# Splitting the mid-kernel loads of a gather-bound layer into transfers of 120 and 8 partitions

## What is computed

```python
h = rmsnorm(x, norm1_g) * (1 + sc1) + sh1
z = h @ w_in                                   # token mixer: SSM and short convolution
x = x + g1 * (mix(z) @ w_out)
h = rmsnorm(x, norm2_g) * (1 + sc2) + sh2
# PEER, per block of 128 tokens: 8 heads, 16 experts of 16384 for each head and token
q = h @ w_query                                # 256 columns for each head
idx, gate = product_key_top_k(q, sub_keys)
hid = einsum("thkd,td->thk", expert_u[idx], h)
act = gelu(hid) * gate
x = x + g2 * einsum("thk,thkd->td", act, expert_v[idx])
y = rmsnorm(x, final_norm_g)
```

## Time and profile before

| | us |
|---|---|
| three runs | 1945.32, 1943.67, 1938.72 |
| median | 1943.67 |
| profiled execution | 1940.8 |
| its span, first to last instruction | 1939.0 |

### The profile page before, as it was taken

One profiled execution on the slowest core, in us unless ns is written; L12 is line 12 of the kernel. 1 busy time (PEld: TensorE's weight loads), 2 busy tenths in 40 slices (PEclk: granted clock), 3 DMA queues, 4 the chain that ended last, 5 costly groups with the idle time before them and its releaser, 6 DMA issues.

```text
span 1939.0 us, 22593 instructions
## 1 busy us (share of the span) xinstructions
PE 1193.7 (62%) x7716; PEld 472.6 (24%) x7716; DVE 1417.4 (73%) x3894; ACT 373.2 (19%) x845; POOL 721.3 (37%) x666
## 2 busy tenths in 40 slices
PE   6999898999767777774643434454444454444434
PEld 3569544444323322220210000111000010110001
DVE  8978567777766776669777777777777778877775
ACT  5242441221122121111210011121111021111010
POOL 0000133333433343435444444444444444444441
PEclk9999999999878777775655555575555565555555
DMA  8555799999999999999999999999999999999994
GB/s 348 182 198 210 274 392 404 371 385 415 403 417 393 403 411 417 409 404 398 421 421 423 421 421 421 421 420 420 423 418 413 421 412 401 420 419 415 413 416 192
DMA packets 126243, 745.91 MB, mean 385 GB/s; under 512 B 12128, under 2 KB 34912, under 8 KB 40624
## 3 DMA queue, kind: packets, MB, share of 16 engines
q0 software_dynamic: 92160, 671.13, 84.0%
q1 hardware_dynamic: 33968, 73.35, 10.6%
HBM read 741.78 MB, written 2.65 MB: 384 GB/s over the span
## 4 chain that ended last, share of the span: by engine, by line
DMA 32%; PE 31%; DVE 24%; issue 10%; ACT 1%; POOL 0%; SPq 0%; DVEq 0%; POOLq 0%; ACTq 0%
DMA r<-table,gidx 21%; DMA mix_r<-table,gidx 8%; DVE r L1718 7%; PE bank L857 7%; PE bank L825 6%; PE bank L962 3%; PE bank L975 2%; PE bank L555 2%; DMA r<-w_query 2%; DMA r<-w_u 2%; DVE mix_r L1718 1%; DVE wgt L1730 1%; PE bank L792 1%; DVE i L1659 1%; DVE r L1685 1%
## 5 line engine op out<-in xcount | busy, mean ns | idle before, releaser
L1904 POOL DMA_INDIRECT r<-table,gidx x542 | 603.2, 1113 | 888.1 <-PE bank L857 711.3
L857 PE MATMUL bank<-r,wgt 128*32 128x512 f32 x2168 | 493.6, 912 | 579.3 <-DVE wgt L1730 579.1
L1718 DVE CUSTOM_DVE_ANT_0 r<-r 128x1024 f32<-128x1024 f32 x542 | 658.9, 1224 | 216.4 <-DMA r<-table,gidx 202.2
L857 PEld LDWEIGHTS bank<-r,wgt 128*32 128x32 f32 x2168 | 56.2, 129 | 882.5 <-DVE wgt L1730 843.2
L1268 ACT ACTIVATE r<-r 128x2 f32<-128x2 f32 x320 | 65.1, 204 | 1019.0 <-DVE r L1718 1018.4
L857 PE MATMUL bank<-mix_r,wgt 128*32 128x512 f32 x392 | 132.6, 982 | 124.0 <-DVE wgt L1730 124.0
L1904 POOL DMA_INDIRECT mix_r<-table,gidx x98 | 109.5, 1118 | 139.1 <-PE bank L857 117.0
L1718 DVE CUSTOM_DVE_ANT_0 mix_r<-mix_r,r 128x1024 f32<-128x1024 f32 x98 | 119.6, 1224 | 42.0 <-DMA mix_r<-table,gidx 39.5
L1727 DVE TENSOR_TENSOR r<-r 128x2 f32<-128x2 f32 x320 | 49.8, 156 | 111.3 <-ACT r L1268 111.3
L825 PE MATMUL bank<-hT_r,r 128*128 128x512 f32 x256 | 119.5, 621 | 0.9 <-ACT hT_r L1122 0.9
L1730 DVE TENSOR_TENSOR wgt<-fold,r 128x64 f32<-128x64 f32 x320 | 72.0, 225 | 11.1
(11 more groups left out here) (360 smaller groups left out, 1506.0 us busy)
## 6 DMA issues: line engine op xcount, KB each, us to landing
r<-w_mod SPq DMA_DIRECT2D x24, 1024.0 KB, 8.6
r<-w_query SPq DMA_DIRECT2D x15, 1024.0 KB, 16.0
r<-table,gidx POOLq DMA_INDIRECT x542, 17.5
r<-w_tiles SPq DMA_DIRECT2D x12, 512.0 KB, 8.3
x_r<-w_tiles SPq DMA_DIRECT2D x10, 512.0 KB, 5.9
hT_r<-xT SPq DMA_DIRECT2D x4, 640.0 KB, 6.2
r<-w_u SPq DMA_DIRECT2D x1, 2048.0 KB, 30.3
r<-w_o SPq DMA_DIRECT2D x1, 2048.0 KB, 10.4
```

The lines of the kernel that those rows point to most:

```text
L857: last = mm(bank[ACC[b % 2][h]][to:to + TG, :], wgt[:, g % 2, e, :], rows[SLOT[G * TOPK + k]][:, D + h * 512:D + (h + 1) * 512], start=(G ...
L1718: V.tensor_tensor_reduce(row, row, h2r[tg], 1.0, 0.0, ALU.mult, ALU.add, hid[:, par, k:k + 1]).then_inc(dot_done, 1)
L1904: G_.indirect_dma_start(rows[SLOT[j]], None, table, bass.IndirectOffsetOnAxis(gidx[:, e, k:k + 1], 0)).then_inc(row_in[SLOT[j]], 16)
```

## The change

Every load that SP asks for behind the first gather, and the stores of `y_out` for blocks 0 to 3, go through a helper that sends partitions 0 to 119 as one DMA and 120 to 127 as a second. Each of the two raises the semaphore by 16, so the waits count in 32s. Bytes, runs, addresses and order are the same, and no other engine has another instruction. The gathers, the loads before 211 us and the last block's two stores stay as they were.

```diff
+WIDE = 120
...
+            def in_two(out, src, sem):
+
+                for p in (slice(0, WIDE), slice(WIDE, P)):
+                    sp.dma_start(out[p], src[p]).then_inc(sem, 16)
+
...
-                sp.dma_start(wqb, w_query[:, :, h * DQ:(h + 1) * DQ]).then_inc(ld_wq, 16)
+                in_two(wqb, w_query[:, :, h * DQ:(h + 1) * DQ], ld_wq)
...
-                sp.dma_start(wtl[slot], w_tiles[n]).then_inc(wtl_in[slot], 16)
+                in_two(wtl[slot], w_tiles[n], wtl_in[slot])
...
-                sp.dma_start(woA[:, m - 4, :, :], w_o[:, m, :, :]).then_inc(wol_in[m - 4], 16)
+                in_two(woA[:, m - 4, :, :], w_o[:, m, :, :], wol_in[m - 4])
...
-                    sp.dma_start(y_out[:, :, 0:P], peer.rearrange("p (k t) -> p k t", k=KD)).then_inc(out_dma, 16)
+                    in_two(y_out[:, :, 0:P], peer.rearrange("p (k t) -> p k t", k=KD), out_dma)
...
-                sp.dma_start(y_out[:, :, b * P:(b + 1) * P], peer.rearrange("p (k t) -> p k t", k=KD)).then_inc(out_dma, 16)
+                in_two(y_out[:, :, b * P:(b + 1) * P], peer.rearrange("p (k t) -> p k t", k=KD), out_dma)
...
-            sp.wait_ge(out_dma, 16 * (NBLK + 1))
+            sp.wait_ge(out_dma, 32 * NBLK)
...
-                pe.wait_ge(ld_wq, 16 * u)
+                pe.wait_ge(ld_wq, 32 * u)
...
-                        pe.wait_ge(wtl_in[(tile + 2) % 3], (tile // 3 + 1) * 16)
+                        pe.wait_ge(wtl_in[(tile + 2) % 3], (tile // 3 + 1) * 32)
...
-                            pe.wait_ge(wol_in[m - 4], 16)
+                            pe.wait_ge(wol_in[m - 4], 32)
...
-                    act.wait_ge(out_dma, b * 16)
+                    act.wait_ge(out_dma, b * 32)
...
-            dve.wait_ge(out_dma, 16 * (NBLK - 1))
+            dve.wait_ge(out_dma, 32 * (NBLK - 1))
```

## The result

The changed kernel takes 2017.58 us in the median of six runs (2012.61 to 2020.45); the kernel before, run beside it on the same chip, 1944.49. The ratio is 1.0374 with a 95% interval of 1.0354 to 1.0393: slower by 73.1 us. The forecast was 1990 us, slower, from 1937 to 2045.

The account below looks back on a forecast made before the run. DMA was taken to bound the gather loop. Loads' time again +67.1, the eighth +8.4, slack -24.2 and stores -4.8 gave +46.5 us on 1940.8, so 1987.3; with 2.9 for the median, 1990 us, range 1937 to 2045.

Parts of the forecast that it names:

- the forecast's first case: Loads beside gathers, 211 to 900 us: rows of another layout contend, costing the loads' time once more; 1990 us, chance 0.57.
- More issues cost nothing: On SP: 35 more DMAs, about 0.33 or 0.54 us each, and doubled semaphore counts add no time.
- The stores' relief: Behind 1000 us: three stores of 1.6 us come off the freed engine, taken as the laggard; -4.8 us.
- The eighth: Loads up to 900 us: the last 8 partitions spread over eight engines, 1/8 more load time on each; +8.4 us.
- The price: Loads beside gathers: rows in a neighbour engine's part of SBUF cost their own time again; +67.1 us, between 0 and 127.
- The slack filled first: Spare DMA time, 14.5 us from 211 to 500 and 9.7 from 500 to 900 us, absorbs added cost first; -24.2 us.
- were to grow by 33 and 18 us: Sign: the stretches 211 to 500 and 500 to 900 us lengthen by 33 and 18 us.
- PE's waits for `w_query` were to be more than two: Sign, 211 to 900 us: later landings make PE wait for `w_query` more than twice, inside the same 46 us.
- POOL was to wait less for PE: Sign, 211 to 900 us: DMA sets the pace, so POOL's waits for PE shrink; no size given.
- nothing meets: Rival for loads beside gathers: no contention, the eighth hidden by slack; -4.8 to +3.6 us, 1939 to 1947; chance 0.27.
- the laggard sets more: Rival: a slow engine also costs 9.7 us between 500 and 900 us; relief up to -14.5 us, about 1932; chance 0.08.
- It does not do what it says: Rival: 120 partitions use 8 engines or fewer, doubling load time there; +43 us, some 1987, without contention; chance 0.08.

Follow-up runs that it names:

- the eleventh experiment: Changed kernel's 120 and 8 split with `w_query` and `y_out` in longer device-memory runs, against the kernel before: 2017.29 us, ratio 1.0379; 76.9 us over that layout unsplit.

## Why the prediction was right, and where its size was off

Slower, by a transfer's rows that meet those of other engines: that was the forecast's first case, and three pairs show it. Column cut against partition cut (+4.5 and +73.1 us), whole against split in the other memory layout (+76.9), and `dskip` with 80 and 128 partitions. By its steps:

1. **More issues cost nothing: nearly held.** The column cut has as many and lies at 1.0021. That is about 4.5 us (0.2 to 8 by its interval), for issues and shorter runs together.
2. **The stores' relief, -4.8 us: fell.** The stores alone gave 1.0001, and the tail of the changed kernel took 914.3 us for 913.4. The count was right (15 engines for 120 partitions, as the packets say), but freeing that one engine brought nothing.
3. **The eighth, +8.4 us: not told apart.** Equal halves cost 69.1, 120 and 8 cost 73.1; the 3.5 us by the ratios have an uncertainty of 7.
4. **The price, once the loads' own time, +67.1 us: near, if none of the slack was used.** Equal halves cost 69.1. That it was taken once, between bounds of 0 and 1.9 times, was a choice and not a result, so there is luck in how near it came. By the packets' time the engines pay 30.5 us more for SP's queue. For all packets together the share and span give 236.1 + 1674.7 = 1910.8 us now; the column cut, with as many transfers, gives 206.5 + 1632.7 = 1839.2. That is +71.6 us between two kernels of the same bytes, whose medians lie 68.6 us apart.
5. **The slack filled first, -24.2 us: the step that missed most.** The runs give two ways to put it. Either nothing of the slack was used and the price was 1.07, 0.98 and 1.09 times the loads' own time (for `w_query` alone, `w_tiles` and `w_o` alone, and all); or it was used, and the price was (50.6 + 24.2) / 47.1 = 1.59, (19.5 + 14.5) / 20.0 = 1.70 and (73.1 + 24.2) / 67.1 = 1.45 times. The first is the more even one. It also fits the sum of the parts: if each of the two had used the slack of the first stretch, 14.5 us, for itself, they would together lie 14.5 us under the whole; they lie 3.0 under it, with some 9 us of uncertainty from the three intervals. The stretches say the same twice. They were to grow by 33 and 18 us and grew by 50 and 28, so that in each about the slack that was put in for it (14.5 and 9.7) is missing. And `w_tiles` and `w_o` alone, 20.0 us of loads, lengthen the first stretch by 24 us, where slack of 14.5 would have left about 6. Over the loads' own time (42.0 and 25.1 us, of which `w_query` has 22.0 and 25.1) the stretches cost 1.19 and 1.12 times in the changed kernel, 1.20 and 1.18 with `w_query` alone, 1.20 with the others. Against the first way stands that the loads with long runs, 11.7 us cheaper, brought only 3.9. The first way is the better supported, and what the 24.2 us were, if not free time, stays open. The warning was in the earlier trace rows: both stretches had a DMA share of 0.99 and 1.00. Here a rate below 421, with engines that are hardly ever without a packet, was not free time that another cost could be put into.

The sum by the first way: equal halves 69.1, the uneven rest 3.5, stores 0, slack 0: 72.6, measured 73.1. That it closes says little, since the first two terms are taken from the time of the halves and its distance to the result. Against the forecast's 46.5 that is +24.2 for the slack, +4.8 for the stores, +2.0 for the price (69.1 for 67.1) and -4.9 for the eighth: 26.1 of the 26.6 us that were missing.

Of the signs named beforehand: the rates were to fall to 353 and 387 GB/s and fell to 336 and 377, and both stretches grew, by more than was given. PE's waits for `w_query` were to be more than two and are eight. The forecast had read the 3.1 and 2.2 us of the earlier trace rows as two waits; they are the two rows of one landing. That these waits lie inside the sum and don't come on top is what the eleventh experiment shows. The tail stayed at 421 and 415. One sign was wrong: POOL was to wait less for PE, since DMA would set the pace. For the same work as in the earlier trace rows, 173.8 us, POOL has in the changed kernel (550 to 978 us), and in the one with long runs and two transfers (546 to 969 us):

```profile
POOL r L1910 <- PE bank L863: 195.6, 45, 12.9
```

```profile
POOL r L1910 <- PE bank L863: 186.8, 48, 7.6
```

PE's lateness for `w_query` can't be all of it, since the second has none of that and its POOL still waits longer than before. POOL waits for the end of a ring that starts with a gather's landing, so that late landings can show there too; how the rest divides is not shown.

Of the rivals, "nothing meets" falls with the result, and "the laggard sets more" with the stores' experiment. "It does not do what it says" falls with the 245 packets, and with equal halves, which load all engines alike and cost the same. The Trainium skill's page "SBUF — State Buffer", section "Door 1: The DMA port swizzle", has the partitions belong to 16 ports in a fixed pattern. The halves, the columns and `dskip` agree with it in direction; no record here names a port, so that the collision at a port remains the explanation that fits, not one that was seen. One rival stands untested: no run has a load of another division with nothing beside it, so part of the price may be that such a load is slower by itself and holds the gathers up behind it.

## What to carry to other kernels

Beside a stream that fills all DMA engines, cut a load by columns and not by partitions: 24 MB of loads in 120 + 8 or 64 + 64 partitions cost 73 and 69 us of 1944, the same loads cut by columns about 4.5 (0.2 to 8). The stores out of SBUF tried here could be cut into 120 + 8 for nothing, but the fullest engine counts and not the sum. When a new wait appears on the critical chain, take it away before you call it the cause: here 45 us of waits for `w_query` went, and the time stayed.

## What the runs showed of the hardware

- A load of 24.1 MB with another division of its partitions, beside gathers of 1.049 MB that alone run at 421 GB/s, cost 3.0 to 3.2 us for each MB, about equally with `w_query` in 1 KB and in 8 KB runs. Both sides pay: SP's packets 30.5 and 35.6 us, the gathers' some 46 and 49 us of each engine.
- Transfers that read SBUF with 120 partitions beside the same gathers cost no more than with 128 (12.7 and 13.2 us for twelve).
- By the packet counts a transfer of 120 partitions leaves one engine out, one of 8 or 7 partitions uses 8 or 7 of them, and 48 stores of 8 and of 7 cost 14.6 and 16.9 us, as much as if all sixteen had had the same load.
- SP's issue of a `w_query` with its 960 or 64 runs of 1 KB took 869 ns in the median and up to 8437 ns in the changed kernel, with 8 KB runs 315 and at most 404 ns.
- One load of 80 partitions beside loads of 128 had the whole core at 289 GB/s in one microsecond (259 to 308 in the thirteen kernels that have it) and 337 over four; with 128 partitions it was at 404 and 411.
